# Projections of the next part run beside each attention step, in a two-block transformer kernel on one core

## The reference

```
h = rmsnorm(x, attn_norm[l]);  proj = h @ w_in[l]
o_a = nsa_attention(...)     # 8 heads of 64 over 2 key groups: compressed, selected and window keys
o_b = diff_attention(...)    # 4 heads, each the difference of two softmaxes, values 128 wide
o_c = chunked_sgu(...)       # gelu, rmsnorm, causal mix within 128 tokens
gates = sigmoid(h @ w_merge[l] + b_merge[l])
x = x + (gates_a*(o_a @ w_branch_a) + gates_b*(o_b @ w_branch_b) + gates_c*(o_c @ w_branch_c)) @ w_out[l]
x = x + (silu(h2 @ w_ffn1[l]) * (h2 @ w_ffn3[l])) @ w_ffn2[l]
```

## Time and profile before

| what | value |
|---|---|
| median of 3 runs | 2436.89 us (2436.76 to 2443.8) |
| the profiled execution | 2437.86 us, its span 2436.1 us |
| busy in the span | PE 89%, weight loads 63%, DVE 47%, ACT 30%, POOL 3% |
| chain that ended last | PE 66%, DMA 16%, DVE 11%, ACT 5% |
| mean granted TensorE clock | 0.955 |

### The profile page before, as it was taken

The page is one execution under the profiler, slowest core; times in us unless marked ns, Lnnn a source line. Parts: engine busy times, 40 slices in busy tenths (PEclk is TensorE's granted clock), DMA queues, the critical chain, the costliest instruction groups (busy, mean ns, idle before and its releaser), DMA issues.

```text
span 2436.1 us, 30759 instructions
## 1 busy us (share of the span) xinstructions
PE 2160.9 (89%) x13048; PEld 1545.5 (63%) x13048; DVE 1148.8 (47%) x1950; ACT 727.3 (30%) x1256; POOL 71.5 (3%) x102
## 2 busy tenths in 40 slices
PE   7977999999978799999996888998997888998998
PEld 7764443333366734333343667998996767998996
DVE  4664232222166623222224565766555565766554
ACT  3731010000034200000002344543443243543442
POOL 2000000000000000000000010010000010010000
PEclk9987999999989899999997999998999999999999
DMA  8117999999951599999996412464453511454551
GB/s 297 70 66 290 428 428 427 428 427 428 418 186 70 224 390 428 427 428 428 427 427 227 173 35 78 165 216 148 160 190 121 196 47 59 163 199 157 188 188 40
DMA packets 127630, 602.47 MB, mean 247 GB/s; under 512 B 5580, under 2 KB 24144, under 8 KB 102784
## 3 DMA queue, kind: packets, MB, share of 16 engines
q1 hardware_dynamic: 122592, 589.32, 61.0%
q10 hardware_dynamic: 3920, 9.97, 1.3%
q0 software_dynamic: 976, 1.15, 0.3%
HBM read 599.37 MB, written 1.05 MB: 246 GB/s over the span
## 4 chain that ended last, share of the span: by engine, by line
PE 66%; DMA 16%; DVE 11%; ACT 5%; issue 1%; ACTq 0%; SPq 0%; DVEq 0%
PE ps L1311 12%; PE ps L414 9%; PE ps L416 9%; PE ps L415 9%; DMA rx<-in_w_up 7%; DMA ring<-in_w_up 7%; PE ps L1346 6%; ACT AB L530 2%; PE ps L427 2%; PE ps L429 2%; PE ps L428 2%; DVE ARm L908 2%; PE ps L2518 2%; PE ps L2519 2%; PE ps L2520 2%; PE ps L1249 1%
## 5 line engine op out<-in xcount | busy, mean ns | idle before, releaser
L396 DVE TENSOR_TENSOR CL<-ring,CH 128x1024 fp32r<-128x1024 f32 x284 | 332.7, 1213 | 276.4 <-ACT CH L390 276.3
L414 PE MATMUL ps<-XTH,CH 128*128 128x256 f32 x1456 | 424.9, 292 | 18.6 <-DVE CL L396 9.5
L415 PE MATMUL ps<-XTL,CH 128*128 128x256 f32 x1456 | 417.0, 286 | 0.0
L416 PE MATMUL ps<-XTH,CL 128*128 128x256 f32 x1456 | 416.7, 286 | 0.0
L390 ACT ACTIVATE CH<-ring 128x1024 fp32r<-128x1024 f32 x284 | 281.8, 1043 | 136.6 <-PE ps L2520 60.8
L414 PEld LDWEIGHTS ps<-XTH,CH 128*128 128x128 f32 x1456 | 284.9, 196 | 22.0 <-DVE XTL L458 9.9
L415 PEld LDWEIGHTS ps<-XTL,CH 128*128 128x128 f32 x1456 | 284.9, 196 | 1.1 <-issue 0.5
L416 PEld LDWEIGHTS ps<-XTH,CL 128*128 128x128 f32 x1456 | 284.6, 195 | 0.0
L1311 PE MATMUL ps<-rx,ARM 128*64 128x512 f32 x1024 | 248.7, 608 | 29.7 <-DMA rx<-in_w_up 20.4
L1311 PE MATMUL ps<-ring,ARM 128*64 128x512 f32 x1024 | 243.9, 601 | 26.1 <-DMA ring<-in_w_up 16.9
L1327 DVE TENSOR_TENSOR ARM<-ARM,ps 128x512 f32<-128x512 f32 x32 | 22.0, 687 | 455.6 <-PE ps L1311 455.6
(11 more groups left out here) (382 smaller groups left out, 3711.9 us busy)
## 6 DMA issues: line engine op xcount, KB each, us to landing
ring<-in_w_gate SPq DMA_DIRECT2D x32, 2048.0 KB, 23.9
ring<-in_w_up SPq DMA_DIRECT2D x32, 2048.0 KB, 26.9
rx<-in_w_down SPq DMA_DIRECT2D x32, 2048.0 KB, 27.1
rx<-in_w_gate SPq DMA_DIRECT2D x32, 2048.0 KB, 26.4
ring<-in_w_down SPq DMA_DIRECT2D x32, 2048.0 KB, 27.1
rx<-in_w_up SPq DMA_DIRECT2D x32, 2048.0 KB, 27.1
ring<-in_w_ffn SPq DMA_DIRECT2D x30, 2048.0 KB, 8.1
ring<-in_w_in SPq DMA_DIRECT2D x14, 2048.0 KB, 8.2
```

The costliest lines, as they stand in the source:

```text
L396: v.e.tensor_tensor(pc.lo[:, cs], pc.ap[:, cs], pc.hi[:, cs].bitcast(F), ALU.subtract).then_inc(dve_done, v.put("lo", pc.k))
L414: p.e.matmul(o, pc.hi[:, c, n0:n0 + 128], src[0][:, c, :], start=c == 0, stop=False)
L415: p.e.matmul(o, pc.hi[:, c, n0:n0 + 128], src[1][:, c, :], start=False, stop=False)
L416: m = p.e.matmul(o, pc.lo[:, c, n0:n0 + 128], src[0][:, c, :], start=False, stop=c == nk - 1)
```

## The change

Seven things are changed.

1. The loops. Scores (maximum, exp) of job 0 stand ahead of the loop; step i does values of job i-1, scores (maximum, exp) of job i+1, then a function `fill(i)`, then transposes (normalise, copy) of job i. All three attentions and both blocks use them; only the second block gives a `fill`.
2. The fill of the NSA jobs is `pe_diff_in`: step i has one `p_feat` for the difference attention's queries and keys and the rotation of the one before; step 8 has the first two value products. The fill of the difference attention's jobs is `pe_sgu_in`: two products a step (values, then the inputs of the third branch).
3. Tile 0's normalisation goes from POOL to DVE, both copies of the transposed tiles to ACT, and the mask product is fp32r (`EYE`, `MASK`) and no longer fp32. The values product alternates the two heads' column halves. Banks are fixed: scores go round three, transposes have two.
4. `pe_hidden` writes its 16 products to four groups of 32 output partitions in turn; a product with `fold` adds the four groups up, and the gelu comes after it.
5. The order within the NSA inputs is new: each rotation stands one product later, keys 0 stand ahead of the first `pe_hidden`, and the compressed probabilities are transposed in the step of job 0.
6. In the second block the ring has three slots; the fourth (`WORK`) holds the difference attention's queries, keys and values, and buffers of the merge.
7. The gelu, squares and roots of the third branch go to the merge's first steps (`act_gelu`, `act_roots`, `dve_sgu`), and its three small loads are issued on ACT's queue ahead of the difference attention's exps.

```diff
+        k = turn[0] % 4
+        into["ring"], WORK = (ring[k:] + ring[:k])[0:3], (ring[k:] + ring[:k])[3].ap
+        turn[0] = 0
...
+                    m = p.e.matmul(o[:, :, 128 * t:128 * t + 128], EYE, bc_mid(MASK, 2), start=False, stop=True)
...
+        def p_attend(jobs, out, fill=nothing):
...
+            p_scores(jobs[0])
+            for i in range(n + 1):
+                if 0 < i < n:
+                    out(jobs[i - 1])
+                if i + 1 < n:
+                    p_scores(jobs[i + 1])
+                fill(i)
+                if i < n:
+                    p_turned(jobs[i])
+                else:
+                    out(jobs[i - 1])
+        def v_attend(jobs, out, fill=nothing):
...
+            v_max(jobs[0])
+            for i in range(n + 1):
+                if 0 < i < n:
+                    out(jobs[i - 1])
+                if i + 1 < n:
+                    v_max(jobs[i + 1])
+                fill(i)
+                if i < n:
+                    v_normed(jobs[i])
+                else:
+                    out(jobs[i - 1])
...
+            keys(0)
+            pe_hidden(l, 0)
+            vals(0)
+            keys_rope(0)
+            pe_hidden(l, 1)
...
-                i = p.e.matmul(b[0:30, 0:256], n.B[k][:, j].rearrange("p g n -> p (g n)"), u.ap[:, j, :], start=j == 0,
-                               stop=j == 15)
+                q = 32 * (j % 4)
+                i = p.e.matmul(b[q:q + 32, 0:256], n.B[k][:, j, :], u.ap[:, j, :], start=j < 4, stop=j > 11)
...
+        def pe_diff_in(l, i):
+
+            d, f = diffs[l], f"in{l}"
+            if i < 8:
+                p_feat(("dqk", l, i), p_piece(f, DIFF + i // 2), (i % 2) * 128, XT, bank=B_FILL)
+            if i:
+                p.wait_ge(act_done, a.at("dqk", l, i - 1))
+                p_rope(("dqk rope", l, i - 1), d.RAW[(i - 1) % 2], B_ROPE)
+            if i == 8:
+                pe_diff_values(l, 0)
+        def dve_diff_in(l, i):
+            d, f = diffs[l], f"in{l}"
+            if i % 2 == 0:
+                v_next(f, DIFF + i // 2)
+            if i:
+                q, j = i - 1, (i - 1) % 4
+                if q < 4:
+                    v_rope(("dqk rope", l, q), d.RAW[q % 2], d.QQ[:, j, :], d.TMP, "dqk in", l, q)
...
+        def pe_sgu_in(l, i):
+
+            f = f"in{l}"
+            if i == 0:
+                pe_diff_values(l, 1)
+            for x in range(2):
+                if 0 < i < 3:
+                    p_toks(("sv", l, i - 1, x), p_piece(f, SGU + i - 1), x, XT, bank=B_FILL + x)
+                elif i > 2:
+                    p_feat(("su", l, 2 * (i - 3) + x), p_piece(f, SGU + i - 1), 128 * x, XT, bank=B_FILL + x)
...
+                    if (n, j) == (0, 0):
+                        act_gelu(l)
+                        a_next(f, PIECE[n][1])
+                        act_roots(l)
```

More of the change, by code:

```diff
@@ L226, in program @@
         turn = [0]
-        into = {}
+        into = dict(ring=ring)
         def begin(name, pool):
@@ L235, in unit @@
         def unit(src, a, n):
-            u = Unit(src, a, n, ring[turn[0] % 4])
+            u = Unit(src, a, n, into["ring"][turn[0] % len(into["ring"])])
             turn[0] += 1
@@ L418, in p_feat, with p_toks @@
             p.name("piece", pc.k)
-        def p_toks(key, pc, t, src, cs=range(8), ready=None):
-            o = take(key)[:, 0:256]
+        def p_toks(key, pc, t, src, cs=range(8), ready=None, bank=None):
+            o = take(key, bank)[:, 0:256]
             for c in cs:
@@ L607, in p_values, with nothing @@
             return m
-        def p_attend(jobs, ready, out):
+        def nothing(i):
+            pass
+        def p_attend(jobs, out, fill=nothing):
             n = len(jobs)
[L611 to L620, removed]
-            n = len(jobs)
[L622 to L630, removed]
@@ L649, in chain, with a_attend @@
+        def a_attend(jobs, out=nothing, fill=nothing):
+            n = len(jobs)
+            a_exp(jobs[0])
+            for i in range(n + 1):
+                if 0 < i < n:
+                    out(jobs[i - 1])
+                if i + 1 < n:
+                    a_exp(jobs[i + 1])
+                fill(i)
+                if i < n:
+                    a_turned(jobs[i])
+                else:
+                    out(jobs[i - 1])
+        def chain(jobs, value):
             for i, j in enumerate(jobs):
-                j.before, j.value, j.of = jobs[i - 2] if i > 1 else None, value[i], of
+                j.before, j.value, j.banks = jobs[i - 2] if i > 1 else None, value[i], (2 * i % 3, (2 * i + 1) % 3)
@@ L1939, in act_nsa @@
             a.wait_ge(pe_done, p.at("gates", l))
-            a.e.activation(n.VTT[0:24, :], tile("gates", l)[0:24, 0:256], ACT.Copy).then_inc(act_done, a.put("gates", l))
+            a.e.activation(n.GV[0:24, :], tile("gates", l)[0:24, 0:256], ACT.Copy).then_inc(act_done, a.put("gates", l))
+            a_next(f, 4)
+            keys(0)
+            hidden(0)
+            vals(0)
             a.wait_ge(pe_done, p.at("gates back", l))
@@ new lines, in act_hidden_back @@
+        def act_hidden_back(l, k):
+            n = nsas[l]
+            b = tile("hidden back", l, k)[:, 0:64].rearrange("p (c m) -> p c m", c=2)
+            a.wait_ge(pe_done, p.at("hidden back", l, k))
+            if k == 0:
+                a.e.activation(n.TK, b[:, :, 0:30], ACT.Gelu_apprx_tanh).then_inc(act_done, a.put("hidden back", l, k))
+                return
+            a.wait_ge(pool_done, g.at("zero nsa", l))
+            for c in range(2):
+                for h in range(2):
+                    a.e.activation(n.TR[:, h, c, :, 0:15], bc_mid(b[:, c, h * 15:h * 15 + 15], 4),
+                                   ACT.Gelu_apprx_tanh).then_inc(act_done, a.put("hidden back", l, k))
@@ L2006, in dve_nsa @@
+            v_next(f, 0)
+            ended(v, *(("ffn", 0) if l else ("moe", 1)))
+            for h in range(2):
+                v.e.tensor_copy(n.W2D[:, :, h, :], n.w2[0]).then_inc(dve_done, v.put("w2d", l))
+            rope(0)
+            v_next(f, 1)
+            rope(1)
+            rope(2)
+            v_next(f, 2)
+            dve_blocks(l, 0)
+            rope(3)
+            dve_blocks(l, 1)
             v_next(f, 3)
```

655 lines of the change are left out of this document (302 added, 353 removed).

## The result

The changed kernel takes 2498.41 us (median of 4 runs, 2494.98 to 2504.02) beside 2438.18 us for the kernel before, measured again with it: 1.0245 times as long, 95% interval 1.0219 to 1.0271. The forecast was 2473, its whole range 2428 to 2508, and the range of the forecast by itself, without its rivals, 2452 to 2492. The profiled execution took 2496.89 us, its span 2495.1, which is 59.0 us more than the span before.

What follows compares the result with a forecast made beforehand. PE, busy in 89% of the span, was taken as the bound. 8.9 for the first block plus 2 x (10.9+3+6.2-6.3) a layer gave +36.5 us on 2437.86: 2473 for the median, range 2428 to 2508.

Steps and rivals of the forecast that it cites:

- rival C: Slower still, 14%: the clock falls in every step, PE's work takes 1.5 to 2 us more in 13 steps, +18 a layer, 2503.
- the merge: Sums and transposed mix weights (1.7+0.6) move in and PE waits some 3.7; with the difference jobs +6.2 a layer.
- the first block's jobs: No fill, so the longer ring shows bare: 6.1 us a step against 4.2, 50.3 against 41.40 us, +8.9, bounds +2 and +12.
- the NSA inputs: Faster hidden layer and fewer waits, less a new wait at keys 0: -6.3 a layer, bounds -15 and 0.
- the difference attention's jobs: Two products beside each job: full steps of 11.45 us, together 51.6 us against 51.43 before.
- The ring: NSA jobs: DVE's normalisation queues behind the new projection's rotation, 10.3 us a step against 8.44; +10.9 a layer.
- The clock: NSA jobs: PE idling 4.2 us in split steps lowers the granted clock, +3 a layer, bounds 0 and +12.
- PE works between: Argument against rival C: PE works between the idle parts of a step (2.1, 0.5 and 0.8 us).
- The wait at keys 0: NSA inputs: with three slots the unit of keys 0 loads late, so PE waits 5.9 us, low clock behind it.
- the stall: Merge: PE's eight banks are full at 15.5, the first sigmoid done near 18.9, so PE waits some 3.7 us.
- A: Faster rival, 10%: projections hide the attention, with DVE's rotation and normalisation running while PE projects; 2360.
- B: About-even rival, 16%: NSA inputs gain -15 a layer; clock, merge and difference jobs at 0; 2438, give or take 10.

Runs made afterwards that it cites:

- e1: The changed kernel with DVE's normalisation of job i moved ahead of fill(i): 2405.74 us, 0.9879 of the kernel before.
- e6: The changed kernel with all nine fills of the NSA jobs run before the jobs, order inside a step untouched: 2463.16 us, 1.0103 of the kernel before.
- e2: The changed kernel with six matmuls that compute nothing in every step, ahead of PE's wait at the transposes: 2477.02 us, 1.0171 of the kernel before.
- e3: The changed kernel with four hidden-layer products in a row to one 32-row group, then the next group: 2506.97 us, 1.0292 of the kernel before.
- e5: e4 with the hidden layer of block 0 ahead of keys 0 and the merge's sums of squares two products earlier: 2365.63 us, 0.9706 of the kernel before.
- e4: The changed kernel with DVE normalising first, PE's scores ahead of values, ACT's exps ahead of copies: 2370.93 us, 0.9731 of the kernel before.
- e7: The changed kernel with the NSA jobs' fills run before the jobs, as in e6, and e4's order inside the steps: 2369.16 us, 0.9724 of the kernel before.

## Why the prediction was right, and which term was too small

The direction, the mechanism and the whole range were right. But 2498 lies above 2452 to 2492, the range of the forecast as laid out, and 5 us under rival C (2503, given 14%): that the sum came within 25 us is in part luck. The NSA jobs with their clock took 11.2 us a layer more than laid out, the merge 3.0, and the first block's jobs 6.8; the NSA inputs and the difference attention's jobs took 3.9 us a layer less each, and made up for 16 of those 35 us.

- **The ring: right.** The rows of the step show each link; e1 broke one link and took 93 us off the kernel after, and e6 showed that apart is shorter than together. At full clock the steps were 10.41 (10.3 laid out) and 5.99 (6.1).
- **The clock: the mis-sized term.** "Some 1 us of PE time for each of three steps: +3" was wrong by a factor of several. From first maximum to first difference scores +25.1 were measured against 13.9, and the clock there was 0.77; if the ring cost its 10.9, the clock cost some 14 and not 3, beyond the bound of 12. What happened is rival C's: the clock fell time after time, also behind the short waits, and not for 1 us in three steps. It fell in the first block too, where the prediction had no clock term at all: +15.7 against +8.9, and e2 brought the clock there to 1.00 and the jobs to 49.2 us, 1.1 under the layout. C's sum, +18 a layer and 2503, came nearest to the time, though C got there with no loss in the first block. The prediction had read in the earlier trace rows how fast the clock falls, and then counted on "PE works between" to keep it up. It did not: it fell behind waits of 2.24 and 0.69 us in the NSA jobs, and of 1.52 and 0.69 in the first block, with PE at work between them.
- **NSA inputs: -10.2 against -6.3.** The hidden layer was put at 3.3 us and took 2.13 and 1.94, some 2.5 us a layer for both. By the Trainium skill, "TensorEngine Tiling (Array Packing)", tiling modes, four such tiles run independently and a change of mode drains the array, which gives an estimate of 1.8 us (7.09/4) and a drain. The trace agrees with the estimate, and no run here shows the drain by itself; by e3 the order of the products decides how much of it is had (7.09, 4.59, 2.0 us). The wait at keys 0 was 5.50 us (5.9 laid out), and it is the third slot's, as the wait for the load shows. The rest of the difference was not taken apart.
- **Difference jobs and merge.** The jobs came to 47.7 us against 51.6 laid out. The two full steps were 10.6 and 12.0 (11.45 each laid out); the difference is in the first step, 11.9 against 13.5, and in the last two, 13.2 against 15.2. The merge grew by 9.0 against 6.0: the stall was 3.68 (3.7 laid out), the sums and transposed weights took 1.7 (2.3 laid out), 1.0 is a new wait for a low half, and the rest goes with a clock of 0.95 over the first 33 us. The stall's place was right and its cause half right: the prediction let the sums and the roots both matter, and e5 shows that the sums do not.
- **The rivals.** A (2360) decides on one point, as stated there: DVE's rotation and normalisation have to run while PE projects. The kernel after fails on it, and e4 (2371) meets it by order alone; but e7 (2369), without any projection beside a job, does as well, so what brought that time is the order and not the hiding. B (2438) needed the NSA inputs at -15 a layer and nothing for the clock; they were -10.2, and the clock cost some 14.
- **First block's start**, 2.4 us later, was put at 1 at most. The experiments do the same work up to there and have it between 752.5 and 755.8 us, so it may be no more than the spread from one execution to the next.

## What to carry to other kernels

When work is put beside a pipelined loop, look at each engine's queue and ask what stands behind the new work although it is ready: here the normalisation stood behind the rotation of the new projection, and one line of order cost 93 us. Put first in each queue what the other engines wait for, and the filler last, as e4 does. On TensorE price a repeated short wait by the granted clock over the whole loop, not for one step. And time the loop with its own order put right before adding anything to hide its latencies: there may be none left.

## What the runs showed of the hardware that was not expected

- With waits of 1.52 and 0.69 us on PE in every step of the first block, the granted clock went up and down, 0.96 in one step and 0.50 in the next, 0.82 over the jobs; six more matmuls ahead of each first wait held it at 1.00 and made the jobs 7.9 us shorter (57.07 to 49.21). With the same instructions in that block, clock and time are not the same in every execution: 0.82 and 57.07 us in the kernel after and in e1, 0.71 and some 62 us in e6. What decides between them was not tried.
- The hidden layer's 32 fp32 records of 256 columns: 2.0 us when neighbouring products (two records each) go to different groups of 32 output rows, 4.6 when four in a row go to the same one, and 7.09 when all go to one group of 30 rows.
